# Attention of a hybrid encoder step: inverse sums on the diagonal that turns the probabilities, half gate pieces ahead of the value products

## What is computed

```python
q = z[..., COL_Q:COL_K].reshape(bn, L, FOX_HEADS, FOX_HEAD_DIM)
...
gates = jax.nn.sigmoid(z[..., COL_GATE:].reshape(bn, L, N_BRANCH, D_MODEL))
...
s = jnp.einsum('bqhd,bkhd->bhqk', qb, k).astype(jnp.float32) * scale
s = s + jnp.transpose(cqb, (0, 2, 1))[..., None] - c_kT[:, :, None, :]
s = jnp.where((k_pos[None, :] <= pb[:, None])[None, None], s, NEG_INF)
p = jax.nn.softmax(s, axis=-1)
return jnp.einsum('bhqk,bkhd->bqhd', p.astype(v.dtype), v)
...
merged = jnp.sum(gates.astype(proj.dtype) * proj, axis=2)
x = x + (merged @ w_out).astype(x.dtype)
```

## Time and profile before

| | us |
|---|---|
| median of three runs | 1898.97 (1897.72 to 1900.55) |
| the profiled execution | 1898.35 |
| its span, first to last instruction | 1896.6 |
| PE busy in it | 1849.6 |
| DVE, ACT, POOL busy | 1195.6, 432.6, 806.1 |
| chain that ended last: share of PE | 40% of the span, all other engines 1% |

### The profile page before, as it was taken

How to read it: one execution, slowest core, us unless ns; L and a number is a source line. 1 busy time by engine, 2 the same in 40 slices (tenths; PEclk the granted TensorE clock), 3 DMA queues, 4 the chain that set the end, 5 groups by cost and what they waited for, 6 DMA issues and landing times. The chain is left out here.

```text
span 1896.6 us, 28821 instructions
## 1 busy us (share of the span) xinstructions
PE 1849.6 (98%) x11323; PEld 1800.7 (95%) x11323; DVE 1195.6 (63%) x1820; ACT 432.6 (23%) x812; POOL 806.1 (43%) x461
## 2 busy tenths in 40 slices
PE   6999999999999999999999999999999999999997
PEld 6989999999989898989999999999999999999997
DVE  6788653888885645542673677557557557557556
ACT  4210122556551111140010231111111111111113
POOL 4434444333356446222232445625625525525530
PEclk9999999999999999999999999999999999999999
DMA  8634829576724454356441111101101101111102
GB/s 272 185 124 130 266 105 262 152 187 172 183 81 142 117 119 100 70 198 229 159 163 45 34 56 56 56 22 55 55 22 55 48 29 55 44 33 55 45 23 97
DMA packets 221949, 203.97 MB, mean 108 GB/s; under 512 B 58305, under 2 KB 200621, under 8 KB 221154
## 3 DMA queue, kind: packets, MB, share of 16 engines
q1 hardware_dynamic: 205650, 170.46, 31.7%
q10 hardware_dynamic: 16208, 32.25, 4.9%
HBM read 138.44 MB, written 59.77 MB: 105 GB/s over the span
## 5 line engine op out<-in xcount | busy, mean ns | idle before, releaser
L154 PE MATMUL bank<-act_hi,w_hi 128*128 128x364 f32 (+2 forms) x2544 | 847.8, 333 | 10.0 <-DVE act_lo L1483 5.2
L154 PE MATMUL bank<-act_lo,w_hi 128*128 128x364 f32 (+2 forms) x2544 | 837.7, 329 | 0.0
L154 PE MATMUL bank<-act_hi,w_lo 128*128 128x364 f32 (+2 forms) x2544 | 837.4, 329 | 0.0
L154 PEld LDWEIGHTS bank<-act_hi,w_hi 128*128 128x128 f32 x2544 | 479.6, 189 | 16.6 <-issue 9.9
L154 PEld LDWEIGHTS bank<-act_lo,w_hi 128*128 128x128 f32 x2544 | 479.3, 188 | 0.9
L154 PEld LDWEIGHTS bank<-act_hi,w_lo 128*128 128x128 f32 x2544 | 478.9, 188 | 0.0
L2771 DVE SCALAR_TENSOR_TENSOR conv<-up_raw,cw,conv 128x1090 f32<-128x1090 f32 x86 | 179.9, 2092 | 63.8 <-ACT up_raw L2657 33.5
L2454 POOL CAST w_hi<-w_raw 128x1024 fp32r<-128x1024 f32 x44 | 47.5, 1079 | 356.9 <-PE bank L154 351.8
L154 PE MATMUL bank<-ffn_hi,down_hi 128*128 128x364 f32 (+2 forms) x528 | 173.9, 329 | 0.8 <-DVE up_raw L2805 0.8
L154 PE MATMUL bank<-ffn_lo,down_hi 128*128 128x364 f32 (+2 forms) x528 | 172.9, 328 | 0.0
L154 PE MATMUL bank<-ffn_hi,down_lo 128*128 128x364 f32 (+2 forms) x528 | 172.7, 327 | 0.0
(11 more groups left out here) (302 smaller groups left out, 2463.1 us busy)
## 6 DMA issues: line engine op xcount, KB each, us to landing
w_raw<-in_w_up SPq DMA_DIRECT2D x44, 512.0 KB, 3.8
w_raw<-in_w_in SPq DMA_DIRECT2D x42, 512.0 KB, 4.7
gate<-gate_scratch ACTq DMA_DIRECT2D x24, 544.0 KB, 4.0
w_raw<-in_w_down SPq DMA_DIRECT2D x22, 512.0 KB, 3.2
gate_scratch<-gate_out ACTq DMA_DIRECT2D x48, 182.0 KB, 2.7
w_raw<-in_w_branch SPq DMA_DIRECT2D x12, 512.0 KB, 4.2
kh<-kh_scratch SPq DMA_DIRECT2D x16, 336.0 KB, 7.2
kl<-kl_scratch SPq DMA_DIRECT2D x16, 336.0 KB, 8.2
```

Of the source, the lines that this page charges most:

```text
L154: mm = pe.matmul(out, w(k), x(k)[:, c0:c0 + cn], start=first and k == ks[0] and n == 0, stop=last and k == ks[-1] and n == 2)
```

## The change

Two things change in `attention_engines`, and nothing elsewhere.

The scaling of the probabilities by the inverse row sum moves into the turning. DVE now multiplies the identity matrix by the inverse sums, row by row, into a new tile `inv_diagonal` (two slots of 128x128), and PE multiplies each block of unscaled `prob` by that diagonal with an ordinary matmul, where it used the transpose form with the identity. The result is the same turned and scaled block. Since the diagonal has two slots, DVE waits for the turning two units back before it writes one.

On PE the gate half of an iteration comes ahead of its value product. On DVE `out_low` moves from ahead of `prob_low` to behind `gate_scale`, and the loop's end is put in the matching order.

```diff
-        mask = sb("mask", [P, P])
+        mask, scale = sb("mask", [P, P]), sb("inv_diagonal", [P, 2, P])
...
                 for k, (c, cn, _) in enumerate(key_blocks(unit(n))):
-                    mm = pe.transpose(pp[0:cn, n % 2, k * P:k * P + nq], prob[0:nq, n % 3, c:c + cn], m.ident[0:nq, 0:nq])
+                    mm = pe.matmul(pp[0:cn, n % 2, k * P:k * P + nq], prob[0:nq, n % 3, c:c + cn], scale[0:nq, n % 2, 0:nq],
+                                   start=True, stop=True)
                 mm.then_inc(turn_done, 1)
...
             for n in range(N + 2):
-                if n in group_of:
-                    pv(group_of[n])
                 if n in half_of:
                     gate_piece(*half_of[n])
                 elif n in piece_of:
                     gate_piece(piece_of[n])
+                if n in group_of:
+                    pv(group_of[n])
...
             def normalise(n):
-                nq, _, nk, _ = extent(n)
+                nq = extent(n)[0]
                 x = n % 3
+                if n >= 2:
+                    dve.wait_ge(turn_done, n - 1)
                 dve.wait_ge(exp_done, n + 1)
                 dve.reciprocal(inv[0:nq, x:x + 1], total[0:nq, x:x + 1]).then_inc(inv_done, 1)
                 dve.wait_ge(inv_done, n + 1)
-                dve.tensor_scalar(prob[0:nq, x, 0:nk], prob[0:nq, x, 0:nk], inv[0:nq, x:x + 1], None,
+                dve.tensor_scalar(scale[0:nq, n % 2, 0:nq], m.ident[0:nq, 0:nq], inv[0:nq, x:x + 1], None,
                                   ALU.mult).then_inc(norm_done, 1)
...
                 if n < N:
                     normalise(n)
-                if n - 1 in group_of and n <= N:
-                    out_low(group_of[n - 1])
                 if 1 <= n <= N:
                     prob_low(n - 1)
                 if n in group_of:
                     out_sum(group_of[n])
+                if n in piece_of and n < N:
+                    gate_scale(piece_of[n])
+                if n - 1 in group_of and n <= N:
+                    out_low(group_of[n - 1])
                 if n >= N:
                     out_low(group_of[n])
-                if n in piece_of:
                     gate_scale(piece_of[n])
                 if n + 2 < N:
                     row_max(n + 2)
```

## The result

| | before | after |
|---|---|---|
| median | 1898.35 us (4 runs) | 1932.03 us (4 runs, 1930.39 to 1932.89) |
| ratio to before | | 1.0176, 95% interval 1.0162 to 1.0189 |
| profiled execution, its span | 1898.35, 1896.6 us | 1930.39, 1928.6 us |

The change makes the kernel 33.4 us slower (0.0176 x 1898.35). Forecast were 1922 and a range of 1910 to 1937: the direction and the range hold, the likeliest value is 10 us too low.

What follows compares the result with a forecast made beforehand. PE's own work, busy 98% of the span, was taken to bound the kernel. Passes +33.9, order's gains -12.4 and its costs +2.0 gave +23.5 us, so 1922 us; the 8-in-10 range was 1910 to 1937.

Steps and rivals of the forecast that it cites:

- the estimate from it: Rival on PE's turning: a block costs 0.44 us, 100 us more, all waits covered, 1980 us; chance 0.03.
- The case that was given 0.80: The forecast itself, for the attention: two passes a block and most waits gone, 1922 us; chance 0.80.
- The passes: PE's turning: a second matmul pass for 288 blocks and 24 small ones, +33.9 us, bounds 32 and 38.
- (a): PE's waits for the low parts of the turned probabilities in the attention: 7.2 us and tails, all 8.3 gained.
- (b): PE's turnings waiting for scaled probabilities: 2.5 us with tails, half taken as gained, 1.2 us.
- (c): PE's wait of 2.2 us at 325.51 for a mask on POOL: longer turning fills 0.9 us of it.
- (d): PE's clock, lowered after the waits of 555 to 560 us: of 3.4 us lost, 2.0 return.
- What the order may cost: Attention: gate halves waiting for their scaling, 1.2 us, and o_lo ahead of the row maximum, 0.8; sum +2.0 us.
- the 0.8 set aside for `o_lo` ahead of the row maximum: DVE's queue: where POOL holds o_lo, the maximum, exp and a later diagonal come late; 0.8 us for all.
- The 1.2 us for the gate's scaling in the middle of the stage: Next gate half waits for a scaling behind the later product's o_sum, 0.3 us at four five-block turnings.
- The second rival: Attention: new waits, o_lo held by POOL ahead of the row maximum, eat the order's gain, +12, 1934; chance 0.12.

Runs made afterwards that it cites:

- The identity experiment: Kernel before with one edit: the turning is an ordinary fp32 matmul with the identity instead of the transpose form; 1925.81 us, ratio 1.015.

## Why the prediction was right, and what in it was wrong

**Right: the bound and the sign.** PE's own work sets the end, the loss lies in the attention, and the stages behind it moved by 0.9 us. The plain matmul is two records at 0.11 us, as lines 2024 and 2043 had shown; the turnings double, from 31.1 to 67.2 us. The Trainium skill, TensorE: Matmul & The Clock Gate, Terms, has transpose mode four times faster for FP32, and the estimate from it was 1980; this case's factor at 128x128 is two. The identity experiment shows that the passes alone bring all that the diagonal half of the change costs. The range held because its upper end allowed for half the gain to fail and for some 6 us of new waits. The case that was given 0.80, most waits gone, is not what came: 8.8 of 11.4 us of waits are left, in other places.

**The passes, forecast 33.9, measured 36.1.** A term that was 2 us small, within its bound of 38.

**(a) The pt_lo waits, forecast 8.3 gained.** They went. (All seven stand behind an `o_lo` that POOL held, the one at 340.52 too; the prediction had six.) But the diagonal alone, in the old order, takes them from 7.2 to 2.4 us: most of this gain came from PE being later, and the new order had little left to win.

**(b) The waits of the turning, forecast 1.2 gained; they grew from 2.0 to 4.7 us.** The prediction named the mechanism, POOL's hold on the diagonal, and halved it where it should have raised it. DVE's scaling shrank to 40.5 us, not 30. Its busy time in after, and the least, median and longest of one in ns:

```profile
310.00:600.00 290.00, 40.52 (x72) 0.99 0.57 145
...
L882 DVE TENSOR_SCALAR inv_diagonal<-ident,row_stats x72: 247/510/2487, 317.0 to 589.3; 128x128 f32<-128x128 f32 x64, 64x64 f32<-64x64 f32 x8
```

The 416 ns of the earlier trace rows were taken as the price of the shape. They are the mean of seven instructions of 0.29 and one of 1.32 that POOL held. The median of the diagonals is 510 ns, because most of them meet a second thing on POOL that the prediction had not read, the mask: it is released by the same row maximum as DVE's next step. 52 of the 72 diagonals start within 0.03 us of a mask addition, and those of 128x128 take 504 to 520 ns; the ten that meet nothing on POOL take 285 to 289 (the one of 64x64 among them 247). At 400.84 and 400.87 both start, and they end within 0.1 us of each other; at 546.32 the diagonal has no mask beside it:

```profile
400.84 0.45 POOL L643 TENSOR_TENSOR nck<-nck,mask 128x128 f32<-128x128 f32 x1 [3.04 <-DVE row_stats L869]
400.87 0.51 DVE L882 TENSOR_SCALAR inv_diagonal<-ident,row_stats 128x128 f32<-128x128 f32 x1
...
546.32 0.29 DVE L882 TENSOR_SCALAR inv_diagonal<-ident,row_stats 128x128 f32<-128x128 f32 x1
```

The Trainium skill, SBUF — State Buffer, SBUF: two separate sides, describes the shared port pair as an exclusive lock. These rows agree, and the 2.49 us above, which end 0.1 us behind POOL's instruction, do too. In the kernel with the diagonal alone, moving it to ACT was worth 7.0 us, though PE's list of waits there showed only 1.3 us for the diagonal and 5.3 in all.

**(c) The wait at 325 us, forecast 0.9 gained:** The earlier trace rows had 2.2, after has 1.1 there. Right.

**(d) The clock, forecast 2.0 gained.** The waits of 555 to 560 us did not go, they stand at 585 to 590 in after, and the clock falls behind them again, for half as long. The stretches of after, where the third number from the end is the clock:

```profile
585.00:590.00 5.00, 2.47 (x17) 2.27 (x16) 4.50 (x10) 2.11 (x6) 3.38 (x2) 0.92 0.33 75
590.00:595.00 5.00, 5.00 (x25) 4.46 (x24) 1.62 (x6) 0.95 (x4) 0.00 (x0) 0.73 0.27 72
```

5 x 0.08 + 5 x 0.27 = 1.8 us against 3.4: 1.6 gained. The dip after 325 us, which the prediction kept, is gone too (1.7 us). These are estimates from one execution each: the traces of the diagonal alone, of the order alone and of the diagonal on ACT have no dip in the attention, that of PE's order alone has the one after 325 and one at 545.

**What the order may cost, forecast 2.0: the step that failed, together with (b).** Added up, the prediction had the order and its waits as 10.4 us of gain; 5.0 came back in the attention, and less than that in the time (36.1 - 33.4 = 2.7). Three terms account for most of the 10 us by which the likeliest value was too low. The waits of the turning grew by 2.7 us where 1.2 less was forecast, and the 0.8 set aside for `o_lo` ahead of the row maximum doesn't cover that. At the stage's end the last two iterations were not followed: there the value product stands between two whole gate pieces with no turning as cover, and the gate waits 2.3 us. The passes were 2.2 us too low. The 1.2 us for the gate's scaling in the middle of the stage were too high instead: with turnings of 0.22 us a block the cover that the prediction worked out is there, and after has one such wait, of 0.3 us. The clock gave back more than forecast, 3.3 us against 2.0.

With the turnings of before the cover is missing, and the same order of PE costs 8.3 us of waits for gate_out and 10 us of time. DVE's queue stands behind the late product: it is idle ahead of o_sum for 34.3 us there and for 44.5 in after, instead of 3.9. The second rival, new waits that eat the order's gain at 1934, had the place of the outcome and a chance of 0.12 only. Its mechanism, o_lo ahead of the row maximum, shows in the longer waits of the turning; on the kernel before, DVE's order by itself is worth nothing, and the costly half is PE's. No run has DVE's order alone on the diagonal.

How the numbers of the parts join is only partly shown. Diagonal +29.0, order +8.5, together +33.4: they share cover, as the experiments on PE's order show (10 us on before, 5.5 with the diagonal on ACT). How much of the 7.0 us from the move to ACT is POOL's hold, and how much DVE's shorter queue, stays open.

## What to carry to other kernels

Where PE is busy throughout, price an edit that makes its matmuls do another engine's work by the records it adds: DVE's 13 us saved here bought nothing that could be measured, PE's 36 us cost 28. Before an instruction is moved behind another to cover one wait, follow what hangs on the instruction that becomes late, on each engine's queue and in the loop's last iterations too; here the gain forecast for the order was a loss of 8.5 us by itself. Where two engines hold each other up, moving the work to a third one with room (ACT, 52% busy in the attention before) gave what no reordering did.

## What the runs showed of the hardware that was not expected

More work on the engine that sets the time can hide its own waits: lengthening PE's work by 36 us in the kernel before cost 28.5, while its pt_lo waits fell from 7.2 to 2.5 us, with no edit to any other engine. And a small DVE instruction between two SBUF tiles took 0.29 us alone and 0.51 beside a POOL instruction of 0.45 that had started 0.03 us earlier, in 52 of 72 cases in after; beside POOL's weight instructions it took up to 2.49 us. The same work on ACT took 0.34 to 0.40 us in all 72.
